# A stick-breaking encoder layer on one core: the down projection in seven products instead of eight, its operands kept in DRAM and moved by GpSimd's queue, and the loops written out

## Chip, core and metric

The kernel runs on one core of one Trainium2 chip. The metric is the device time of one execution in microseconds (us): for the kernel before, the median of 3 runs is 2521.99 us (2521.57 to 2523.63).

## What is computed

One encoder layer for 528 prompt rows (16 of them learned meta rows) and 32 sample rows, all in float32. Only the last part, the SwiGLU block, is touched in its arithmetic:

```python
def layer(h, attend, conv_state, w_in, w_out, ...):          # h: rows x 2048
    xn = rms_norm(h, g_pre_mix); proj = xn @ w_in            # 6144 columns: q k v, gate_b gate_c conv_in
    attn = attend(q, k, v)                                   # stick-breaking attention, 8 heads of 128
    conv_y = short_conv(gate_c * conv_in, conv_state, conv_w)
    mix = concat(group_rms_norm(attn), group_rms_norm(gate_b * conv_y))
    h = h + rms_norm(mix @ w_out, g_post_mix)
    xf = rms_norm(h, g_pre_ffn)
    ff = silu(xf @ w_gate) * (xf @ w_up)                     # w_gate, w_up: 2048 x 5632
    return h + rms_norm(ff @ w_down, g_post_ffn)             # w_down: 5632 x 2048
```

## The kernel before

**Layout.** Activations are kept transposed: 128 channels on the partitions, rows along the free axis. The feed-forward part works on 544 rows (the meta rows are dropped), as two halves of `TH` = 272. Every float32 operand of TensorE is split into a rounded part (`_hi`, made by ScalarE) and a rest (`_lo`, made by VectorE), and each product of a 128x128 weight block is three matmuls: hi x hi, hi x lo, lo x hi.

**Order of the program.** Input projection and mixers (loops `Fori` over pairs of heads and of channel groups), output projection (a loop over pairs of output chunks), then the feed-forward part, in which every instruction is already written out: 44 *steps* of gate and up, then down. Each engine runs its own list in order and waits on semaphores; the order on each engine is written by hand.

**Gate and up: seven products.** A step makes one 256-column block of `w_gate` (even step) or `w_up` (odd step) times the activations, in the Winograd form of Strassen's scheme: the 2x2 blocks of weights and of activations are combined so that 7 products of half-size blocks take the place of 8. The seven products of a step are called, in order, B11, B21, T2, T3, T1, T4, B22. B blocks come straight from the loaded panel, T blocks are differences that VectorE makes (`combine`). Each product uses a tile of 128x1024 weights: ScalarE rounds it (`tile_high`), VectorE makes the rest (`tile_rest`), TensorE then runs 24 matmuls of 272 columns (`product`, line 955). There are 4 tile slots (`RING_T`), so the tile of a product is made only when the product four before it is done. The quarters of the result are finished on VectorE as `c11`, `c22`, `c21`, with the help of copies (`m1`, `u2`, `m7`) that ScalarE takes out of PSUM. Product B22 adds onto the PSUM bank that `c22` reads, so TensorE waits for `c22_made` before B22, the last product of a step.

**The hidden activations.** After an odd step, in the next even step, VectorE multiplies up by gate into `hid` (2 x 544 per partition), ScalarE rounds it to `hid_hi` (`round_hidden`), VectorE makes `hid_lo` (`hidden_rest`), and SyncE stores both to DRAM (`store_hidden`, 2 x 544 KB, lines 573 and 574).

**Down: eight products' worth.** `down_tiles` are 88 tiles of 512x256 weights (`down_raw`, 512 KB), in 4 batches over the 5632 hidden channels. A tile takes 48 matmuls of 272 columns (line 1004). The hidden operand of a batch, `ffs`, is loaded back from DRAM (line 600, 1088 KB each) in bursts on SyncE's queue, ahead of weight tiles on the same queue. At the end of a batch VectorE adds PSUM into `y` (`take_down`, line 1855). In the last batch ScalarE squares finished chunks of `y` and GpSimd adds the squares up (line 1893) for the last norm; the residual `h2_back` (4352 KB) is loaded on SyncE's queue (line 626).

## Time and profile before

| | |
|---|---|
| median of 3 runs | 2521.99 us |
| the profiled execution | 2524.61 us, its span 2522.9 us |
| mean granted TensorE clock | 0.981 |
| TensorE matmul busy | 2440.0 us (97%) |
| VectorE, ScalarE, GpSimd busy | 1252.4, 915.5, 99.0 us |
| moved by DMA | 290.66 MB, mean 115 GB/s |

The span is one execution by the hardware profiler. In rows of groups, the busy time of a matmul group counts overlapping matmuls more than once, since one starts every 0.126 us and lasts 0.29 us; the pace is read from a count over a stretch. An instruction on VectorE or ScalarE lets the next one start some 0.08 to 0.09 us before its own end is recorded.

### The profile page before, as it was taken

How to read it: one execution, taken by the hardware profiler on the slowest of the kernel's cores; microseconds unless marked ns; L12 is line 12 of the kernel's file. 1: busy time of each engine (PE TensorE's matmuls, PEld its weight loads, DVE VectorE, ACT ScalarE, POOL GpSimd, SP SyncE). 2: the span in 40 equal slices, each digit the busy share in tenths (PEclk: the TensorE clock that was granted, in tenths of full speed). 3: DMA queues.
4: the chain of work that ended last, by engine and by line, in shares of the span. 5: the costliest groups of instructions: out<-in, count | busy, mean ns of one | idle time of the engine just before them, and what ended most of it. 6: DMA issues, size and time to landing. Idle time of an engine off the chain costs nothing.

```text
span 2522.9 us, 43292 instructions
## 1 busy us (share of the span) xinstructions
PE 2440.0 (97%) x18716; PEld 2394.1 (95%) x18716; DVE 1252.4 (50%) x1387; ACT 915.5 (36%) x1177; POOL 99.0 (4%) x155
## 2 busy tenths in 40 slices
PE   8999999999999985999999999999999999999997
PEld 7999999999999984999999999999999999999996
DVE  5324332444353228777777767676765222222144
ACT  6344444422342224444444444444443111111123
POOL 0000000000011100000000000000000000000024
PEclk9999999999999996999999999999999999999997
DMA  7223222232225321434343434333336516242222
GB/s 235 83 64 89 80 80 65 85 92 84 80 70 167 89 75 64 134 119 136 118 137 118 137 118 136 119 131 124 126 129 262 187 43 232 76 171 85 105 93 71
DMA packets 313049, 290.66 MB, mean 115 GB/s; under 512 B 8348, under 2 KB 296500, under 8 KB 309956
## 3 DMA queue, kind: packets, MB, share of 16 engines
q1 hardware_dynamic: 298528, 281.70, 34.5%
q10 hardware_dynamic: 14372, 6.77, 0.9%
q8 instruction: 118, 1.93, 0.3%
q14 instruction: 31, 0.25, 0.0%
HBM read 245.82 MB, written 42.61 MB: 114 GB/s over the span
## 4 chain that ended last, share of the span: by engine, by line
PE 90%; DVE 5%; DMA 2%; ACT 2%; SPq 1%; issue 1%; POOL 0%; POOLq 0%; ACTq 0%; DVEq 0%
PE ps L955 36%; PE ps L422 30%; PE ps L1004 19%; PE ps L722 4%; DMA down_raw<-in_w_down_dram 2%; DVE xs L1716 1%; PE ps L666 1%; DMA misc<-in_x_sample_dram 0%; DVE misc L1720 0%; DVE y_left L1880 0%; DVE wide L1685 0%; DVE misc L1689 0%; DVE y_right L1880 0%; ACT xs L1320 0%; DVE t_lo L1695 0%
## 5 line engine op out<-in xcount | busy, mean ns | idle before, releaser
L955 PE MATMUL ps<-xs,t_hi 128*128 128x272 f32 x4928 | 940.5, 291 | 33.1 <-DVE xs L1716 19.1
L955 PEld LDWEIGHTS ps<-xs,t_hi 128*128 128x128 f32 x4928 | 780.9, 190 | 34.7 <-issue 32.2
L955 PE MATMUL ps<-xs,t_lo 128*128 128x272 f32 x2464 | 716.6, 291 | 0.0
L1004 PE MATMUL ps<-ffs,t_hi 128*128 128x272 f32 x2816 | 470.7, 290 | 12.7 <-DVE y_right L1855 7.3
L955 PEld LDWEIGHTS ps<-xs,t_lo 128*128 128x128 f32 x2464 | 467.3, 190 | 0.0
L1695 DVE TENSOR_TENSOR t_lo<-panel,t_hi 128x1024 fp32r<-128x1024 f32 x261 | 319.4, 1224 | 255.7 <-ACT t_hi L1313 255.7
L422 PE MATMUL ps<-act_hi,w_hi 128*128 128x272 f32 (+1 forms) x2048 | 435.4, 294 | 3.5 <-DVE act_lo L1532 2.3
L422 PE MATMUL ps<-act_lo,w_hi 128*128 128x272 f32 (+1 forms) x2048 | 427.0, 290 | 0.0
L422 PE MATMUL ps<-act_hi,w_lo 128*128 128x272 f32 (+1 forms) x2048 | 426.8, 290 | 0.0
L1004 PEld LDWEIGHTS ps<-ffs,t_hi 128*128 128x128 f32 x2816 | 402.2, 190 | 13.4 <-issue 7.5
L1313 ACT CAST t_hi<-panel 128x1024 fp32r<-128x1024 f32 x261 | 272.8, 1045 | 191.8 <-PE ps L955 185.4
L422 PEld LDWEIGHTS ps<-act_hi,w_hi 128*128 128x128 f32 x2048 | 322.8, 189 | 7.5 <-DVE act_lo L1532 3.0
L422 PEld LDWEIGHTS ps<-act_hi,w_lo 128*128 128x128 f32 x2048 | 324.2, 189 | 0.0
L422 PEld LDWEIGHTS ps<-act_lo,w_hi 128*128 128x128 f32 x2048 | 323.8, 189 | 0.0
L1004 PE MATMUL ps<-ffs,t_lo 128*128 128x272 f32 x1408 | 293.3, 290 | 0.0
L1791 DVE TENSOR_TENSOR t_lo<-down_raw,t_hi 128x1024 fp32r<-128x1024 f32 x88 | 109.8, 1248 | 304.1 <-ACT t_hi L1358 304.1
L408 DVE TENSOR_TENSOR w_lo<-w_raw,w_hi 128x1024 fp32r<-128x1024 f32 x126 | 157.9, 1254 | 192.2 <-ACT w_hi L402 190.7
L1358 ACT CAST t_hi<-down_raw 128x1024 fp32r<-128x1024 f32 x88 | 92.2, 1048 | 403.2 <-PE ps L1004 305.8
L402 ACT CAST w_hi<-w_raw 128x1024 fp32r<-128x1024 f32 x128 | 133.7, 1046 | 282.8 <-PE ps L422 222.1
L1004 PEld LDWEIGHTS ps<-ffs,t_lo 128*128 128x128 f32 x1408 | 221.7, 190 | 0.0
L1346 ACT ACTIVATE m<-ps 128x272 f32<-128x272 f32 x88 | 34.9, 397 | 150.1 <-PE ps L955 150.1
L1313 ACT CAST t_hi<-t_raw 128x1024 fp32r<-128x1024 f32 x44 | 46.2, 1049 | 69.3 <-PE ps L955 69.3
(174 smaller groups left out, 1547.1 us busy)
## 6 DMA issues: line engine op xcount, KB each, us to landing
w_raw<-in_w_in_dram SPq DMA_DIRECT2D x96, 512.0 KB, 3.8
panel<-in_w_up_dram SPq DMA_DIRECT2D x44, 1024.0 KB, 5.1
down_raw<-in_w_down_dram SPq DMA_DIRECT2D x88, 512.0 KB, 5.2
panel<-in_w_gate_dram SPq DMA_DIRECT2D x43, 1024.0 KB, 6.4
w_raw<-in_w_out_dram SPq DMA_DIRECT2D x32, 512.0 KB, 3.9
ff_hi_scr<-hid_hi SPq DMA_DIRECT2D x22, 544.0 KB, 2.7
ff_lo_scr<-hid_lo SPq DMA_DIRECT2D x22, 544.0 KB, 4.4
ffs<-ff_hi_scr SPq DMA_DIRECT2D x11, 1088.0 KB, 11.7
```

What stands on the lines that cost most here:

```text
L402: nc.scalar.copy(w_hi[:, k % SLOTS, :], raw_slot(k)).then_inc(hi_ready, 1)
L408: engine.tensor_tensor(w_lo[:, k % SLOTS, :], raw_slot(k), w_hi[:, k % SLOTS, :].bitcast(F32), ALU.subtract).then_inc(lo_ready, 1)
L422: mm = nc.tensor.matmul(out[:, h, :], w[:, k, col:col + width], x[:, x_at + k, token + h * half:token + (h + 1) * half], start=begins, sto ...
L666: return nc.tensor.transpose(out, src, ident[0:n, 0:n])
L722: return nc.tensor.matmul(out, w, x, start=start, stop=True, skip_group_check=True)
L955: mm = nc.tensor.matmul(out, w[:, k, :], xs[:, x, part, k, :], start=begins and k == 0 and w is hi and part == 0, stop=k == KH - 1 and w i ...
L1004: mm = nc.tensor.matmul(ps[:, 4 * (pair % 2) + 2 * n + h, 0:TH], w[:, k, n * P:(n + 1) * P], ffs[:, b % 2, u, part, k, h * TH:(h + 1) * TH ...
L1313: nc.scalar.copy(tile_of(t_hi, i), raw_tile(i)).then_inc(tile_hi, 1)
L1346: A(out[:, :], step_bank(step, letter), ACT.Copy).then_inc(made, 1)
L1358: nc.scalar.copy(down_tile_of(t_hi, i), down_raw[d % 6][:, :, :]).then_inc(tile_hi, 1)
L1695: V.tensor_tensor(tile_of(t_lo, i), raw_tile(i), tile_of(t_hi, i).bitcast(F32), ALU.subtract) .then_inc(tile_lo, 1)
L1791: V.tensor_tensor(down_tile_of(t_lo, i), down_raw[d % 6][:, :, :], down_tile_of(t_hi, i).bitcast(F32), ALU.subtract).then_inc(tile_lo, 1)
```

## The change

1. **Down in seven products.** Down becomes 24 steps (`DSTEPS`): 6 batches of 4 or 3 pairs of hidden chunks (`KBS`), 4 column blocks each. A step has the same seven products as gate and up, each with a tile of 128x1024 (batches of 4) or 128x768 (batches of 3), and 24 or 18 matmuls of 272 columns. Weights come through the same panels as gate and up (`load_panel`, 1 MB or 0.75 MB), and VectorE makes four differences for each step as before. After every product VectorE takes 2x272 columns out of PSUM into `y` (`take_down`), since the next product adds on in the same bank.
2. **Seven hidden operands.** Down needs seven combinations of the hidden quarters, not two. VectorE makes four more quarters (`hidden_sums`), and rounding, rest and stores work on 7x272 = 1904 elements per partition instead of 1088. Each store is 128 x 7 pieces of 1088 bytes, 0.975 MB; two for each pair of steps. `hid_lo` now lies on top of `hid`, so `c11` of an odd step waits until the stores have landed (`hid_stored`).
3. **Places.** `round_hidden` moves behind the `m7` copy in the even step, `hidden_rest` to the odd step behind `combine(T4)`, and `c11` of odd steps behind the tile of B22.
4. **Queue.** Stores and loads of hidden operands are issued by GpSimd; loads of `xd` (12 slots, 2 x 544 KB each) begin as products of the last step free their room, and later follow the last use of a slot.
5. **Loops.** Every `Fori` becomes a Python loop.

```diff
-        with sp.Fori(0, HEADS // 2 - 1) as r:          # and so for all engines and loops
+        for r in range(0, HEADS // 2 - 1):
...
+    KBS = [4, 4, 4, 4, 3, 3]
+    NQ = KC // 4
+    DSTEPS = NQ * len(KBS)
+    ALL = STEPS + DSTEPS
+    XD = 12
...
             def round_hidden(j):
-                act.wait_ge(hid_made, j + 1)
+                act.wait_ge(hid_summed, 4 * (j + 1))
                 if j:
                     act.wait_ge(hid_stored, 32 * j)
                 nc.scalar.copy(hid_hi[:, :, :], hid[:, :, :]).then_inc(hid_rounded, 1)
...
-                if is_gate and step:
-                    round_hidden(j - 1)
                 copy_out(u2, step, T2, "a", u2_copied, c21_made)
                 tile_high(7 * step + 6)
                 copy_out(m7, step, T3, "b", m7_copied, c22_made)
+                if is_gate and step:
+                    round_hidden(j - 1)
                 tile_high(ahead)
...
             def c11(step):
-                if step >= 2:
-                    dve.wait_ge((hid_made, hid_split)[step % 2], step // 2)
+                if step >= 2 and step % 2 == 0:
+                    dve.wait_ge(hid_made, step // 2)
+                if step >= 3 and step % 2:
+                    dve.wait_ge(hid_stored, 32 * (step // 2))
...
+            def hidden_sums(j):
+                d21, d11, d12, d22, s1, s2, s4 = (hid[:, h, :] for h in range(7))
+                dve.wait_ge(hid_made, j + 1)
+                V.tensor_tensor(s1, d21, d22, ALU.add).then_inc(hid_summed, 1)
+                dve.wait_ge(hid_summed, 4 * j + 1)
+                V.tensor_tensor(d21, d11, d21, ALU.subtract).then_inc(hid_summed, 1)
+                V.tensor_tensor(s2, s1, d11, ALU.subtract).then_inc(hid_summed, 1)
+                dve.wait_ge(hid_summed, 4 * j + 3)
+                V.tensor_tensor(s4, d12, s2, ALU.subtract).then_inc(hid_summed, 1)
...
+            for d in range(DSTEPS):                      # TensorE
+                b, m = d // NQ, d % NQ
+                for q in range(7):
+                    i = 7 * (STEPS + d) + q
+                    slot = (7 * b + q) % XD
+                    pe.wait_ge(tile_lo, i + 1)
+                    if m == 0:
+                        pe.wait_ge(xd_loaded[slot], 32 * ((7 * b + q) // XD + 1))
...
+                    in_y = {B11: 7 * (d - 1), B21: 7 * (d - 1) + 2, T2: 7 * d + 1, T3: 7 * (d - 1) + 6,
+                            T1: 7 * d + 3, T4: 7 * d + 4, B22: 7 * d + 5}[q]
+                    if in_y > 0:
+                        pe.wait_ge(y_added, in_y)
+                    for n in range(2):
+                        for k in range(KBS[b]):
+                            for w, part in ((hi, 0), (hi, 1), (lo, 0)):
+                                mm = nc.tensor.matmul(out[:, n, :], w[:, k, n * P:(n + 1) * P], xd[:, slot, part, k, :], ...
...
+            def store_hidden(j):                         # GpSimd
+                pool.wait_ge(hid_split, j + 1)
+                for part, src in enumerate((hid_hi, hid_lo)):
+                    pool.dma_start(ff_scr[part][:, :, j, :], src[:, :, :].bitcast(F32)).then_inc(hid_stored, 16)
...
+            for j in range(FF // 2 - 1):
+                store_hidden(j)
+            for i in range(XD):
+                pool.wait_ge(product_done, 7 * LAST + i // 2 + 1)
+                load_hidden(i)
+            store_hidden(FF // 2 - 1)
+            for i in range(XD, 7 * len(KBS)):
+                b, q = (i - XD) // 7, (i - XD) % 7
+                pool.wait_ge(product_done, 7 * (STEPS + NQ * b + NQ - 1) + q + 1)
+                load_hidden(i)
```

The order of instructions moves at three places. First, ScalarE's list in an even (gate) step, from the copy of `u2` or the tile ahead of it to the first two tiles of the next step (`m`, `u` are the copies `m1`, `m7`, `u2`; panels carry a buffer number). Before:

```order
L1313 CAST t_hi<-panel_69 128x1024
L1352 CAST hid_hi<-hid 128x1088
L1346 ACTIVATE u_73<-ps 128x272
L1313 CAST t_hi<-panel_69 128x1024
L1346 ACTIVATE m_74<-ps 128x272
L1313 CAST t_hi<-panel_70 128x1024
L1313 CAST t_hi<-panel_68 128x1024
```

After:

```order
L1332 ACTIVATE u_73<-ps 128x272
L1299 CAST t_hi<-panel_69 128x1024
L1332 ACTIVATE m_74<-ps 128x272
L1338 CAST hid_hi<-hid 128x1904
L1299 CAST t_hi<-panel_70 128x1024
L1299 CAST t_hi<-panel_68 128x1024
```

The rounding of the hidden operand stood ahead of the copy of `u2`; now it stands behind the `m7` copy and directly ahead of the tile of the next step's B11, and it is 1904 elements wide instead of 1088.

Second, VectorE's list in the same even step, from the tile of T4 to `c22` (which is `gate<-ps,m_74`). Before:

```order
L1695 TENSOR_TENSOR t_lo<-panel_69,t_hi 128x1024
L1759 TENSOR_TENSOR gate<-ps,m_72 128x272
L1695 TENSOR_TENSOR t_lo<-panel_69,t_hi 128x1024
L1786 TENSOR_TENSOR hid_lo<-hid,hid_hi 128x1088
L1695 TENSOR_TENSOR t_lo<-panel_70,t_hi 128x1024
L1708 TENSOR_TENSOR panel_70<-panel_70 128x8x128
L1764 TENSOR_TENSOR gate<-ps,m_74 128x272
```

After:

```order
L1674 TENSOR_TENSOR t_lo<-panel_69,t_hi 128x1024
L1741 TENSOR_TENSOR gate<-ps,m_72 128x272
L1674 TENSOR_TENSOR t_lo<-panel_69,t_hi 128x1024
L1769 TENSOR_TENSOR hid<-hid 128x272
L1771 TENSOR_TENSOR hid<-hid 128x272
L1772 TENSOR_TENSOR hid<-hid 128x272
L1774 TENSOR_TENSOR hid<-hid 128x272
L1674 TENSOR_TENSOR t_lo<-panel_70,t_hi 128x1024
L1688 TENSOR_TENSOR panel_70<-panel_70 128x8x128
L1747 TENSOR_TENSOR gate<-ps,m_74 128x272
```

The rest of the hidden operand left this step, and four sums of 272 elements stand in its place. They come ahead of the tile of the next step's B11.

Third, VectorE's list in the next odd (up) step, from the tile of T3 to `c22` (here `hid<-ps,m_74`). Before:

```order
L1695 TENSOR_TENSOR t_lo<-panel_70,t_hi 128x1024
L1708 TENSOR_TENSOR panel_68<-panel_68,t_raw 128x8x128
L1695 TENSOR_TENSOR t_lo<-panel_70,t_hi 128x1024
L1695 TENSOR_TENSOR t_lo<-panel_68,t_hi 128x1024
L1759 TENSOR_TENSOR hid<-ps,m_72 128x272
L1695 TENSOR_TENSOR t_lo<-panel_68,t_hi 128x1024
L1695 TENSOR_TENSOR t_lo<-panel_69,t_hi 128x1024
L1708 TENSOR_TENSOR panel_69<-panel_69 128x8x128
L1764 TENSOR_TENSOR hid<-ps,m_74 128x272
```

After:

```order
L1674 TENSOR_TENSOR t_lo<-panel_70,t_hi 128x1024
L1688 TENSOR_TENSOR panel_68<-panel_68,t_raw 128x8x128
L1778 TENSOR_TENSOR hid_lo<-hid,hid_hi 128x1904
L1674 TENSOR_TENSOR t_lo<-panel_70,t_hi 128x1024
L1674 TENSOR_TENSOR t_lo<-panel_68,t_hi 128x1024 x2
L1741 TENSOR_TENSOR hid<-ps,m_72 128x272
L1674 TENSOR_TENSOR t_lo<-panel_69,t_hi 128x1024
L1688 TENSOR_TENSOR panel_69<-panel_69 128x8x128
L1747 TENSOR_TENSOR hid<-ps,m_74 128x272
```

The rest of the hidden operand now stands ahead of the tiles of T1 and T4, and `c11` (`hid<-ps,m_72`), which carries the wait for the stores, behind the tile of B22; the tile of the next B11, `combine(T1)` and `c22` stand behind it.

## Rows read from the trace of the kernel before

**Rows 1.** The page: busy time by engine; the chain that ended last, by line

```profile
PE 2440.0 (97%) x18716; PEld 2394.1 (95%) x18716; DVE 1252.4 (50%) x1387; ACT 915.5 (36%) x1177; POOL 99.0 (4%) x155
...
PE ps L955 36%; PE ps L422 30%; PE ps L1004 19%; PE ps L722 4%; DMA down_raw<-in_w_down_dram 2%; DVE xs L1716 1%; PE ps L666 1%; DMA misc<-in_x_sample_dram 0%; DVE misc L1720 0%; DVE y_left L1880 0%; DVE wide L1685 0%; DVE misc L1689 0%; DVE y_right L1880 0%; ACT xs L1320 0%; DVE t_lo L1695 0%
```

**Rows 2.** Stretches: us, busy of PE, PEld, DVE, ACT, POOL (x instructions), clock, DMA, GB/s

```profile
40.00:860.00 820.00, 816.17 (x6179) 790.67 (x6179) 302.64 (x415) 314.13 (x376) 45.82 (x113) 1.00 0.30 89
1100.00:1970.00 870.00, 870.00 (x6903) 870.00 (x6902) 609.89 (x640) 374.94 (x500) 0.00 (x0) 1.00 0.42 142
```

**Rows 3.** The chain in order of time, down and the end

```profile
1937.94 144.34 PE ps L1004 x1152
...
2085.43 17.78 DMA down_raw<-in_w_down_dram
...
2380.07 14.79 DMA down_raw<-in_w_down_dram
...
2485.82 0.73 DVE y_right L1855
2486.58 0.67 ACT y_sq L1122
```

**Rows 4.** PE's waits, 2000 to 2523 us

```profile
PE ps L1004 <- DVE y_right L1855: 7.3, 1, 7.3
PE ps L1004 <- DVE t_lo L1791: 5.3, 1, 5.3
```

**Rows 5.** Groups by form: busy us, mean ns of one, idle before

```profile
L1695 DVE TENSOR_TENSOR t_lo<-panel,t_hi 128x1024 fp32r<-128x1024 f32 x261 | 319.4, 1224 | 255.7 <-ACT t_hi L1313 255.7
...
L1313 ACT CAST t_hi<-panel 128x1024 fp32r<-128x1024 f32 x261 | 272.8, 1045 | 191.8 <-PE ps L955 185.4 <-DMA panel<-in_w_up_dram 6.5
...
L1893 POOL TENSOR_TENSOR y_sq_sum<-y_sq_sum,y_sq 128x544 f32<-128x544 f32 x14 | 19.0, 1354 | 63.9 <-ACT y_sq L1122 63.8
...
L1855 DVE TENSOR_TENSOR y_right<-ps,y_right 128x544 f32<-128x544 f32 x24 | 17.3, 724 | 44.8 <-PE ps L1004 44.8
...
L1716 DVE TENSOR_TENSOR xs<-misc,xs 128x2176 fp32r<-128x2176 f32 x6 | 14.4, 2422 | 3.9 <-ACT xs L1320 3.9
...
L1320 ACT CAST xs<-misc 128x2176 fp32r<-128x2176 f32 x6 | 11.9, 2004 | 20.6 <-DVE misc L1746 9.0 <-DVE misc L1720 6.9 <-DVE t_lo L1695 4.7
```

**Rows 6.** Timeline of DVE: start us, duration us, line, operation

```profile
1525.83 1.28 DVE L1786 TENSOR_TENSOR hid_lo<-hid,hid_hi 128x1088 fp32r<-128x1088 f32 x1
1527.72 1.23 DVE L1695 TENSOR_TENSOR t_lo<-panel,t_hi 128x1024 fp32r<-128x1024 f32 x1 [0.60 <-ACT t_hi L1313]
1528.86 1.22 DVE L1708 TENSOR_TENSOR panel<-panel 128x1024 f32<-128x1024 f32 x1
1529.99 0.43 DVE L1764 TENSOR_TENSOR gate<-ps,m 128x272 f32<-128x272 f32 x1
...
1537.94 1.22 DVE L1708 TENSOR_TENSOR panel<-panel,t_raw 128x1024 f32<-128x1024 f32 x1
1539.82 1.23 DVE L1695 TENSOR_TENSOR t_lo<-panel,t_hi 128x1024 fp32r<-128x1024 f32 x1 [0.67 <-ACT t_hi L1313]
```

**Rows 7.** Timeline of ACT, the same steps

```profile
1526.64 1.04 ACT L1313 CAST t_hi<-panel 128x1024 fp32r<-128x1024 f32 x1
...
1535.43 0.40 ACT L1340 ACTIVATE gate<-ps 128x272 f32<-128x272 f32 x1 [1.65 <-PE ps L955]
```

**Rows 8.** Timeline of SP's DMA issues, the same steps

```profile
1527.19 0.34 SPq L573 DMA_DIRECT2D ff_hi_scr<-hid_hi  x1
1527.57 0.43 SPq L574 DMA_DIRECT2D ff_lo_scr<-hid_lo  x1
1528.05 13.41 SPq L560 DMA_DIRECT2D panel<-in_w_gate_dram  x2
```

**Rows 9.** Stretches with transfers, columns as in rows 2

```profile
1527.75:1534.50 6.75, 6.75 (x56) 6.75 (x55) 6.75 (x8) 3.08 (x5) 0.00 (x0) 1.00 0.94 317
1942.00:1946.00 4.00, 4.00 (x34) 4.00 (x33) 1.67 (x2) 1.05 (x1) 0.00 (x0) 1.00 1.04 397
```

**Rows 10.** DMA issues of line 600: ns min/median/max

```profile
L600 SPq DMA_DIRECT2D ffs<-ff_hi_scr x11: 319/432/5236, 1919.8 to 2235.5; - x11
```

**Rows 11.** The page's DMA issues: KB each, us to landing

```profile
panel<-in_w_up_dram SPq DMA_DIRECT2D x44, 1024.0 KB, 5.1
...
ff_hi_scr<-hid_hi SPq DMA_DIRECT2D x22, 544.0 KB, 2.7
```

More of the change, by code:

```diff
@@ L582, in _ @@
                     sp.wait_ge(tile_lo, T1 + 1)
-                if step > 3 and step % 2 == 0:
-                    store_hidden(step // 2 - 2)
                 load_panel(step, 0)
@@ L889, in _ @@
                 head(0, u, u, u > 0, False)
-            with pe.Fori(1, HEADS // 2) as p:
+            for p in range(1, HEADS // 2):
                 for u in range(2):
@@ L894, in _ @@
                 group(HEADS // 2, u, HEADS + u, first_pair=True)
-            with pe.Fori(HEADS // 2 + 1, (HEADS + GROUPS) // 2) as p:
+            for p in range(HEADS // 2 + 1, (HEADS + GROUPS) // 2):
                 for u in range(2):
@@ L930, in _ @@
             two_chunks(T_OUT, mix_chunk, 2, {6: last_norm_and_rows})
-            with pe.Fori(1, KC // 2) as q:
+            for q in range(1, KC // 2):
                 for c in range(2):
@@ L1246, in _ @@
                 head(0, u, u, u > 0, False)
-            with act.Fori(1, HEADS // 2) as p:
+            for p in range(1, HEADS // 2):
                 for u in range(2):
@@ L1251, in _ @@
                 group(HEADS // 2, u, HEADS + u, first_pair=True)
-            with act.Fori(HEADS // 2 + 1, (HEADS + GROUPS) // 2) as p:
+            for p in range(HEADS // 2 + 1, (HEADS + GROUPS) // 2):
                 for u in range(2):
@@ L1294, in _ @@
             out_round(0, 2)
-            with act.Fori(1, KC // 2 - 1) as q:
+            for q in range(1, KC // 2 - 1):
                 out_round(q, 0)
@@ L1635, in _ @@
                 head(0, u, u, u > 0, False)
-            with dve.Fori(1, HEADS // 2) as p:
+            for p in range(1, HEADS // 2):
                 for u in range(2):
@@ L1640, in _ @@
                 group(HEADS // 2, u, HEADS + u, first_pair=True)
-            with dve.Fori(HEADS // 2 + 1, (HEADS + GROUPS) // 2) as p:
+            for p in range(HEADS // 2 + 1, (HEADS + GROUPS) // 2):
                 for u in range(2):
@@ L1673, in _ @@
             out_round(0, 2)
-            with dve.Fori(1, KC // 2 - 1) as q:
+            for q in range(1, KC // 2 - 1):
                 out_round(q, 0)
@@ L1802, in _ @@
                     x_rest(S3, 6, a21)
+                if step % 2 and step > 1:
+                    hidden_rest(step // 2 - 1)
                 tile_rest(7 * step + 4)
@@ L1818, in _ @@
                     c11(step)
+                if step % 2:
+                    c11(step)
                 if after_up:
-                    hidden_rest(step // 2 - 1)
-                if step < LAST:
+                    hidden_sums(step // 2 - 1)
+                tile_rest(ahead)
+                combine(step + 1, T1)
+                c22(step)
+                combine(step + 1, T2)
+                tile_rest(ahead + 1)
+                c21(step)
+                combine(step + 1, T3)
+                tile_rest(ahead + 2)
@@ new lines, in _ @@
+            for d in range(DSTEPS):
+                step = STEPS + d
+                ahead = 7 * (step + 1)
+                more = step + 1 < ALL
+                if d:
+                    take_down(d - 1, B22)
+                tile_rest(7 * step + 3)
+                combine(step, T4)
+                if d == 0:
+                    times_gate(LAST)
+                if d == 1:
+                    hidden_rest(FF // 2 - 1)
+                take_down(d, B11)
+                tile_rest(7 * step + 4)
+                if d == 0:
+                    times_gate_rest(LAST)
+                take_down(d, B21)
+                tile_rest(7 * step + 5)
+                take_down(d, T2)
+                tile_rest(7 * step + 6)
+                if d == 0:
+                    hidden_sums(FF // 2 - 1)
+                take_down(d, T3)
+                if more:
@@ L1925, in mask @@
                 last.then_inc(ready, 1)
-            with pool.Fori(1, HEADS + 1) as heads:
+            for heads in range(1, HEADS + 1):
                 mask(relu, sp_made, sp_ready, heads)
```

299 lines of the change are left out of this document (120 added, 179 removed).

## The prediction

> **What bounds the kernel now.** I read the page first: TensorE is busy 97% of the span, and nine tenths of the chain that ended last are its matmuls [rows 1]. A busy PE can hide small gaps, so the next view is the windows: from 1100 to 1970 us, inside gate and up, PE is busy 870 of 870 us with 6903 matmuls, 0.126 us each, at clock 1.00 [rows 2]. So a product of 24 matmuls takes 3.02 us and a step of 168 takes 21.17 us. VectorE (610 of 870 us) and ScalarE (375) follow. Whatever removes matmuls gains, and whatever makes PE wait between products loses, one for one. The chain in order of time shows down from 1937.94 to 2485.82 us, 547.9 us [rows 3]; its 4224 matmuls at 0.126 are 532 us, and PE waited 7.3 and 5.3 us [rows 4], once behind a burst of hidden operands and once behind the residual, each time with `down_raw` late on the same queue [rows 3]. The sum is made against the profiled execution's parts (span 2522.9, own time 2524.61) and applied to the median 2521.99, 2.6 us below it.
>
> **Down itself.** Seven products of 2 x K x 3 matmuls, 4 column blocks, the K adding up to 22: 7 x 2 x 3 x 22 x 4 = 3696 matmuls, 528 fewer. At 0.126 us, with the same 272 columns, 465.7 us. Is VectorE able to follow? A 1024-wide operation starts 1.14 us after the one before it (1527.72 to 1528.86 [rows 6]); one of 272 takes 0.35 by the same slope, the 544 taken out of PSUM 0.64 (0.724 recorded [rows 5], less the 0.08 overlap). A step of K = 4 asks 7 rests, 4 differences and 7 takes: 11 x 1.14 + 7 x 0.64 = 17.0 us of 21.17. A step of K = 3 (768 wide, 0.87): 11 x 0.87 + 7 x 0.64 = 14.0 of 15.9. The tightest slot holds a take, a rest and a difference: 2.92 of 3.02 us, and 2.38 of 2.27 us for K = 3. There VectorE slips 0.1 us a slot, plus 0.5 where the rest must first wait for ScalarE's rounding, and gains it back in the three slots without a difference. PE needs a take only two products after its own, so with K = 3 it may be 1.6 us late; I find at most 0.8. No stall. The two old waits go too: weights and hidden operands no longer stand behind each other in one queue. The residual still goes ahead of panels, 11 us at 397 GB/s [rows 9], but a panel is issued about 16 us ahead of its use.
>
> At the start of down the first seven slots (7.8 MB) are issued behind the last store, together with three panels; at 350 to 397 GB/s they arrive 0 to 5 us late for the last product of the first step; I take 2. The sums and the rounding of the last hidden pair stand in this step as well, 1.2 us. Down: 465.7 + 3.2 - 547.9 = **-79.0**.
>
> **The end.** Before, the last take (0.73) and one square (0.67) stand between the last product and the norm [rows 3]. Now the last product finishes two chunks, and the two before them are done one product (2.27 us) earlier: four additions on GpSimd at 1.35 us each [rows 5] run into the end. T4's take and first square end 1.0 us before the last product, two additions bring it to +1.7, the third to +3.1, against 1.4 now: **+1.7**.
>
> **Loops.** Between 40 and 860 us, where most loops run, PE is idle 3.8 us in all [rows 2]. Written out they give 0 to 3.8; code that is written out already runs without a gap from 1100 us on, so I add no price for it. **-0.5**.
>
> **Even steps: a new wait behind the sums.** The even step shown ends at 1535.4 (ScalarE answers B22 at 1535.43 [rows 7]), so its B22 starts at 1532.35. Today `c22` runs at 1529.99 and ends at 1530.42 [rows 6], 1.9 us early. In the change four sums start where the rest stood, at 1525.83. Two wait for an earlier one's end (0.43 + 0.06), so the last ends at 1527.6. ScalarE then rounds 1904 elements: between 1045 ns for 1024 and 2004 for 2176 [rows 5] that is 1.78 us, 1.69 until the next may start. The tile of the next B11 starts at 1529.35 instead of 1526.64 [rows 7]. Behind it, one after the other without slack, stand the rest, `combine(T1)` and `c22` [rows 6]. So `c22` ends at 1533.13, and B22 waits **0.83 us**. 21 even steps: **+17.4**. Its bounds are 0.5 and 1.2 (a semaphore wait more or less on each hop), 10 to 25 us.
>
> **Odd steps: the store.** VectorE comes 1 to 2 us late out of the even step, so `combine(T4)`, 2.5 us after the step's start now (1537.94 [rows 6]), runs at about 3.0, and the rest of 1904 elements (2.13 us, between 1.22 and 2.42 [rows 5]) ends at 6.25. Then two stores of 0.975 MB go out. `c11` waits for both, and behind it in VectorE's list stand the tile of the next B11, `combine(T1)` and `c22`: 0.35 + 1.14 + 1.14 + 0.43 + 0.1 of hops = 3.2 us. B22 starts at 18.15. So the stores have 8.7 us from the end of the rest; each microsecond more costs PE one, 21 times.
>
> How long do they take? Before, two stores of 0.557 MB and one panel half (1.05 MB) share the engines: 317 GB/s from 1527.75 to 1534.5, ramps included [rows 9], first bytes some 0.8 us after the issue at 1527.19 [rows 8]. In the change the panel half is issued by SyncE 1.1 us behind the stores (its condition, the tile of T1, is next in VectorE's list), and runs beside them on the other queue, so it must be moved before the stores are through: 3.0 MB. At 397 GB/s, the rate of large pieces [rows 9], this is 7.6 us, at 317 it is 9.5. I take 350, 8.6 us, since the pieces are 1088 bytes: more than the weights' 1024, less than the 4352 of the old stores. With 0.1 for the hop, 0.8 to the first byte, 0.5 for a queue that no row shows and 0.3 for the end: 10.3 us, **1.6 us** late, 21 times: **+33.6**. Bounds: 8.5 us (no wait at all, +0), and 13.3 us, if each of GpSimd's issues of 896 pieces takes as long as the longest issue of line 600, 5.24 us [rows 10], and a landing of 2.7 [rows 11] follows: 4.6 us late, +97.
>
> The Trainium skill (DMA: Bandwidth & Descriptors, Anatomy of one DMA) gives 2.0 us + bytes / 436 GB/s for a DMA issued from GpSimd, and calls the making of descriptors small. By it, 3.0 MB would be through in 8.9 us, 0.2 us late, and the whole kernel at an estimated 2466 us: the rival below called "hidden". No row here shows a DMA issued by GpSimd. The same page (Issuing engines are not separate DMA queues) says that all queues run on the same 16 engines, so that another issuer saves issue time only; it speaks for counting the panel with the stores.
>
> **Sum.** -79.0 + 1.7 - 0.5 + 17.4 + 33.6 = -26.8: **2495 us**, 1.1% less.
>
> **Rivals.**
> - *Hidden* (25%): the stores are through in under 9.3 us, because they and the panel run at the 397 GB/s of large pieces. For it: in down the old queue held 397 GB/s over 4 us with weights and hidden operands mixed [rows 9]. Then the odd steps cost 0 to 13 us: 2521.99 - 79.0 + 1.7 - 0.5 + 17.4 = 2462 to 2475.
> - *GpSimd is slow to issue* (25%), the case on the other side: seven pieces for each partition, 896 in each of the two DMAs, must be written out before the engines can move them, and SyncE's issues do not show this cost. It decides from 11.6 us on, where 21 waits of 2.9 us eat the whole gain: 2523. At 13.3 us the time is 2559. Against it: SyncE issues the 1024 pieces of a panel half with no such delay, and it lands in 5.1 us [rows 11].
> - *Down is bound by VectorE* (5%): each take or semaphore hop 0.2 us dearer than the rows give, so that the K = 3 steps fall behind: 8 steps by 1 to 2 us, 10 to 16 us more than forecast, 2505 to 2511.
> - The rest, 45%, is the forecast, 2478 to 2515.
>
> **How the numbers follow.** Runs of one kernel differ by under 0.1%, a comparison can tell about 0.2%, 5 us. Slower by more than that is the upper part of the slow issuer, 24%; within it, where forecast and slow issuer meet (2517 to 2527), 7%; faster 69%. The range: 2458 (hidden, with all of the loops' 3.8 us) to 2560 (the upper bound of the stores). It holds both sides, since the stores' time multiplies by 21.
>
> **What the profile would show.** Right: 3696 matmuls in down in about 470 us at full busy; in gate and up, PE idle 0.8 us before the last product of even steps, released by `gate<-ps,m`, and 1 to 2 us before that of odd steps, released by `hid<-ps,m`; VectorE's `c11` in odd steps waiting on the transfer into `ff_lo_scr`, 10 us after GpSimd's issue. Wrong: a landing far from 10 us; a step of 21.2 us or of more than 24; PE waiting for `y_left`, `y_right` or `xd` within down. The forecast falls if GpSimd's queue delays more than the 0.5 us given it, or if the engines serve the stores before the panel.

## The result

The changed kernel takes **2606.18 us** (median of 4 runs, 2602.51 to 2609.05) against 2522.81 (2521.57 to 2525.19) for the kernel before on the same chip: ratio **1.0328**, 95% interval 1.031 to 1.0347. It is slower by 83 us where 27 us less were forecast, and the time lies above the range. The profiled execution of the changed kernel has a span of 2600.8 us; the differences below are made against the 2522.9 of before.

The page of the changed kernel, busy time by engine, then the chain by line (they answer to [rows 1]):

```profile
PE 2424.8 (93%) x18188; PEld 2369.7 (91%) x18188; DVE 1553.0 (60%) x1755; ACT 1009.2 (39%) x1257; POOL 189.3 (7%) x283
...
PE ps L427 29%; PE ps L938 15%; PE ps L995 15%; DMA ff_lo_scr<-hid_lo 9%; PE ps L705 4%; DVE t_lo L1674 4%; DVE panel L1688 3%; ACT t_hi L1299 3%; DVE hid_lo L1778 2%; DMA panel<-in_w_down_dram 1%; PE ps L649 1%; POOL ff_hi_scr L1953 1%; DVE xs L1696 1%; DVE misc L1700 0%; DVE y_left L1888 0%
```

The matmuls of gate and up (now line 938) no longer hold the chain alone: 9% of it is a transfer, the second store of the hidden operand. TensorE's waits in the changed kernel (in total, times, longest) say where:

```profile
PE ps L938 <- DVE hid L1747: 82.3, 21, 6.7
...
PE ps L938 <- DVE gate L1747: 18.1, 21, 0.9
```

These are the waits for `c22`, from the end of the last matmul to the start of the next, in the odd steps (3.9 us each; 1.6 forecast) and in the even ones (0.86 each; 0.83 forecast). What `c22` is late for in an odd step is in VectorE's waits, and in the page's DMA issues (KB each, us to landing; before: [rows 11]):

```profile
DVE hid L1741 <- DMA ff_lo_scr<-hid_lo: 143.8, 20, 9.9
```

```profile
panel<-in_w_gate_dram SPq DMA_DIRECT2D x43, 1024.0 KB, 7.2
...
ff_hi_scr<-hid_hi POOLq DMA_DIRECT2D x22, 952.0 KB, 6.1
ff_lo_scr<-hid_lo POOLq DMA_DIRECT2D x22, 952.0 KB, 11.5
```

One odd step in time, first VectorE, then GpSimd, then SyncE's queue (start, duration):

```profile
1521.08 2.14 DVE L1778 TENSOR_TENSOR hid_lo<-hid,hid_hi 128x1904 fp32r<-128x1904 f32 x1
...
1536.12 0.44 DVE L1741 TENSOR_TENSOR hid<-ps,m 128x272 f32<-128x272 f32 x1 [7.12 <-DMA ff_lo_scr<-hid_lo]
```

```profile
1523.54 0.91 POOL L1953 DMA_DIRECT2D ff_hi_scr<-hid_hi  x1 [45.03 <-DVE hid_lo L1778]
1524.27 1.11 POOL L1953 DMA_DIRECT2D ff_lo_scr<-hid_lo  x1
```

```profile
1524.38 0.37 SPq L585 DMA_DIRECT2D panel<-in_w_gate_dram  x1
1529.02 0.37 SPq L585 DMA_DIRECT2D panel<-in_w_up_dram  x1
```

The rest ends at 1523.2, the store has landed at 1536.0: **12.8 us**, where 10.3 were forecast. GpSimd begins its first issue 0.3 us after the rest and takes 0.7 us to the next; from then to the landing it is 11.7 us. Behind `c11` the tail of 3.2 us is as forecast (1536.12 to TensorE's restart at 1539.33).

The second thing is in the granted clock. Stretches of TensorE around this wait (us, busy of PE, PEld, DVE, ACT, POOL, then clock, DMA share, GB/s), with the long stretches that answer to [rows 2]:

```profile
1100.00:1970.00 870.00, 787.52 (x5916) 780.84 (x5915) 579.55 (x635) 347.78 (x442) 33.03 (x36) 0.95 0.38 124
1535.40:1539.30 3.90, 0.04 (x1) 0.01 (x1) 3.18 (x5) 0.79 (x1) 0.00 (x0) 0.88 0.41 143
1539.30:1545.00 5.70, 5.67 (x25) 5.70 (x26) 4.77 (x5) 1.05 (x1) 0.00 (x0) 0.50 0.01 3
2200.00:2300.00 100.00, 100.00 (x795) 100.00 (x795) 82.60 (x85) 34.69 (x33) 7.47 (x14) 1.00 0.55 184
```

After 3.9 us without a matmul, TensorE works for 5.7 us at a clock of 0.50, the level of 1.2 GHz: 25 matmuls where the usual pace gives some 45. The page shows this as busy time, which is why "93% busy" and "5916 matmuls in 870 us instead of 6903" are both true.

What the slow clock costs can be read from one wait to the next. In gate and up a wait stands before every B22, so 168 matmuls lie between TensorE's restart after one wait and the start of the next wait. Behind the short waits of even steps this takes 21.42 us each time. Behind the waits of two odd steps it took (the clock is the mean of the stretch):

```profile
1539.33:1563.35 24.02, 24.02 (x168) 23.80 (x168) 16.05 (x20) 10.22 (x12) 0.00 (x0) 0.88 0.28 89
1589.12:1612.06 22.94, 22.93 (x168) 22.72 (x168) 16.05 (x20) 10.23 (x12) 0.00 (x0) 0.93 0.29 92
```

The same reading for all 21 odd steps gives 1.3 to 2.7 us beyond 21.42, **41.3 us** in all, 2.0 for each pair of steps.

**Where the 78 us are.** Down starts at 2088.40 instead of 1937.94, 150.5 us later. Of this, 82.3 + 18.1 are the waits above. The 50 us left are not waits; 41.3 of them are the slow clock, the rest is placed further below. Down then takes from 2088.40 to 2556.9, 468.5 us instead of 547.9: -79.4. From the last product to the end it is 43.9 us instead of 37.1: +6.8. Sum: 150.5 - 79.4 + 6.8 = 77.9, the difference of the spans.

### The profile page after: what moved, and what is told of

Its sections match the earlier page's. It is cut to its first block, busy times and chain, and to the rows that moved or that the text cites. A ratio compares the mean times of both kernels' runs of the same rounds, so it can differ in the third digit from the quotient of the medians.

```text
span 2600.8 us, 42070 instructions
## 1 busy us (share of the span) xinstructions
PE 2424.8 (93%) x18188; PEld 2369.7 (91%) x18188; DVE 1553.0 (60%) x1755; ACT 1009.2 (39%) x1257; POOL 189.3 (7%) x283
## 4 chain that ended last, share of the span: by engine, by line
PE 64%; DVE 15%; DMA 11%; ACT 5%; issue 5%; POOL 1%; SPq 0%; DVEq 0%; ACTq 0%; POOLq 0%
PE ps L427 29%; PE ps L938 15%; PE ps L995 15%; DMA ff_lo_scr<-hid_lo 9%; PE ps L705 4%; DVE t_lo L1674 4%; DVE panel L1688 3%; ACT t_hi L1299 3%; DVE hid_lo L1778 2%; DMA panel<-in_w_down_dram 1%; PE ps L649 1%; POOL ff_hi_scr L1953 1%; DVE xs L1696 1%; DVE misc L1700 0%; DVE y_left L1888 0%
## 5 line engine op out<-in xcount | busy, mean ns | idle before, releaser
L938 PE MATMUL ps<-xs,t_hi 128*128 128x272 f32 x4928 | 983.5, 299 | 132.4 <-DVE hid L1747 82.3
L938 PEld LDWEIGHTS ps<-xs,t_hi 128*128 128x128 f32 x4928 | 813.8, 198 | 141.8 <-issue 139.4
L1674 DVE TENSOR_TENSOR t_lo<-panel,t_hi 128x1024 fp32r<-128x1024 f32 (+1 forms) x405 | 486.1, 1200 | 232.7 <-ACT t_hi L1299 226.6
L1299 ACT CAST t_hi<-panel 128x1024 fp32r<-128x1024 f32 (+1 forms) x405 | 412.1, 1023 | 492.2 <-PE ps L995 232.6
L995 PE MATMUL ps<-xd,t_hi 128*128 128x272 f32 x2464 | 466.4, 289 | 3.6 <-DVE y_left L1839 1.5
L995 PEld LDWEIGHTS ps<-xd,t_hi 128*128 128x128 f32 x2464 | 387.3, 188 | 4.9 <-issue 4.9
L995 PE MATMUL ps<-xd,t_lo 128*128 128x272 f32 x1232 | 356.6, 289 | 0.0
L995 PEld LDWEIGHTS ps<-xd,t_lo 128*128 128x128 f32 x1232 | 231.7, 188 | 0.0
L1299 ACT CAST t_hi<-t_raw 128x1024 fp32r<-128x1024 f32 (+1 forms) x68 | 69.7, 1025 | 145.4 <-DVE t_raw L1688 110.1
L1953 POOL DMA_DIRECT2D ff_hi_scr<-hid_hi x22 | 20.0, 910 | 1136.1 <-DVE hid_lo L1778 1136.1
```

The costliest lines, as they stand in the source:

```text
L938: mm = nc.tensor.matmul(out, w[:, k, :], xs[:, x, part, k, :], start=begins and k == 0 and w is hi and part == 0, stop=k == KH - 1 and w i ...
L995: mm = nc.tensor.matmul(out[:, n, :], w[:, k, n * P:(n + 1) * P], xd[:, slot, part, k, :], start=q in (B11, B21, T3) and k == 0 and w is h ...
L1299: nc.scalar.copy(tile_of(t_hi, i), raw_tile(i)).then_inc(tile_hi, 1)
L1674: V.tensor_tensor(tile_of(t_lo, i), raw_tile(i), tile_of(t_hi, i).bitcast(F32), ALU.subtract)\
L1953: pool.dma_start(ff_scr[part][:, :, j, :], src[:, :, :].bitcast(F32)).then_inc(hid_stored, 16)
```

## The experiments

The expectations speak of theories. The main one: the stores of an odd step land later than forecast, the long wait lowers the clock as well, and together they eat the gain of down; all else went as forecast. What lengthens the landing was then divided into "bytes beside a panel half" (D) and "GpSimd's many pieces by themselves" (E). Each kernel is the changed one with the edit shown, unless told otherwise.

### Who issues: stores on SyncE's queue

```diff
                 load_panel(step, 0)
+                if step % 2 == 0 and 4 <= step <= STEPS + 2:
+                    store_hidden(step // 2 - 2)          # SyncE; GpSimd's is gone
```

> The changed kernel with one thing undone: the two stores of the hidden operand are issued by SyncE, ahead of the second panel half of the next step, instead of by GpSimd. Theory A (the loss is the wait of c11 in odd steps for the stores, 3.9 us each, and the lower clock that follows it, about 2.4 us each, 21 times, and it comes from sharing the engines with two panel halves and from GpSimd's later start): in one queue the stores go first, land 6 to 8 us after the rest is made, the wait and the low clock go, 2606 - 21 x 6.3 = about 2474 us. Rival B (the amount moved in that window decides, whoever issues it): the landing stays over 10 us and the time over 2550 us. Rival C (the panel halves behind the stores come late instead): ScalarE waits for the panel, 2480 to 2520 us.

2501.71 us, ratio to before 0.9915 (0.9898 to 0.9931): the gain is there, but less than the 2474 of the main theory. Its trace, the second store's issues, then TensorE's waits:

```profile
ff_lo_scr<-hid_lo SPq DMA_DIRECT2D x22, 952.0 KB, 7.7
```

```profile
PE ps L945 <- DVE hid L1754: 20.1, 5, 19.0
```

In the odd steps the second store lands 7.7 us after its issue and TensorE hardly waits (1.1 us in the other four waits together). One wait of 19.0 us stands at the last step ahead of down, where this kernel issues the last stores while GpSimd's 24 loads of hidden operands are under way (1940 to 1985 us):

```profile
xd<-ff_lo_scr POOLq DMA_DIRECT2D x12, 544.0 KB, 17.0
...
ff_lo_scr<-hid_lo SPq DMA_DIRECT2D x1, 952.0 KB, 27.3
```

So this edit does two things: it puts the panel half behind the stores in one queue, and it opens a new collision. It doesn't say which of issuer and order mattered. The time lies in the range of rival C, but not for its reason: the late step is that of the last stores, not a step with a late panel half.

### Who waits: `c22` of odd steps in a buffer of its own

```diff
-                if step >= 3 and step % 2:                                 # in c11
-                    dve.wait_ge(hid_stored, 32 * (step // 2))
...
+                out = up22[:, :] if step % 2 else quarter(gate, 1, 1)      # in c22
...
+                if step >= 3 and step % 2:                                 # in c21
+                    dve.wait_ge(hid_stored, 32 * (step // 2))
...
-                if step % 2:
-                    c11(step)                        # behind the tile of B22
...
                 c21(step)
+                if step % 2:
+                    c11(step)
```

> The changed kernel, GpSimd still issuing, with the wait moved off the path: in odd steps c22 goes into a spare buffer, c11 stands behind c21, and c21 carries the wait for the stores. Theory A: the stores still take 12 to 13 us, but nothing waits for long; no wait of TensorE in odd steps, clock 1.00, about 2474 us. Rival: if transfers by GpSimd slow the kernel in another way (panel halves late, ports), more than 20 us of the 132 stay, over 2495 us.

**2480.05 us**, ratio 0.983 (0.9814 to 0.9846). The stores are as slow as before (the trace shows 11.6 us), but nothing on TensorE's way waits for them, and the clock stays at 1.00 from 1100 to 1935 us. TensorE's waits for `c22`:

```profile
PE ps L939 <- DVE gate L1747: 18.6, 22, 0.9
```

Against the changed kernel, 126 us: 21 waits of 3.9 us are 82 of them. This shows that the whole loss hangs on that one wait, and that the other 44 us of it are no waiting time: with the wait gone, the slow clock goes as well.

### The wait shortened: `c11` two entries later

```diff
-                if step % 2:
-                    c11(step)
...
                 tile_rest(ahead)
                 combine(step + 1, T1)
+                if step % 2:
+                    c11(step)
                 c22(step)
```

> The changed kernel, in which c11 of odd steps, with its wait for the stores, stands behind the tile of the next B11 and combine(T1) instead of ahead of them. TensorE's wait should fall from 3.9 to about 1.7 us each, 21 times. If the lower clock after it follows from any wait of this kind, 2606 - 46 = about 2560 us; if a wait of 1.7 us leaves the clock at 1.00, as the 0.86 us of even steps does, about 2606 - 46 - 50 = 2510 us.

2522.47 us, ratio 0.9996 (0.9985 to 1.0008). The wait is not removed, only shortened:

```profile
PE ps L938 <- DVE hid L1747: 37.1, 21, 4.3
```

```profile
1100.00:1970.00 870.00, 820.73 (x6382) 813.48 (x6381) 625.76 (x684) 374.18 (x475) 34.94 (x38) 0.99 0.41 135
```

21 waits of 1.8 us on average instead of 3.9 save 45.2 us of waiting, but 83.7 us of time; of the spans, 2600.8 - 2524.0 = 76.8. The other **31.6 us** are slow clock that this kernel is spared, but it isn't spared all of it, as the mean of 0.99 says. After two of its waits, of 1.5 and of 2.3 us, the 168 matmuls took

```profile
1089.36:1110.78 21.42, 21.42 (x168) 21.20 (x168) 16.05 (x20) 10.24 (x12) 0.00 (x0) 1.00 0.32 101
1135.37:1158.28 22.91, 22.91 (x168) 22.68 (x168) 16.05 (x20) 10.22 (x12) 0.00 (x0) 0.93 0.28 94
```

In six of the 21 odd steps the clock fell to 0.50 for a while, after waits of 1.8 to 4.3 us; after the other 15, of 1.0 to 1.7 us, it stayed at 1.00. The length alone doesn't decide: it also stayed at 1.00 after single waits of 2.5 us (the last kernel but one below, at 1939.7) and 2.8 us (the one with long runs, at 1974.1). The six cost 8.8 us, 1.3 to 1.5 each. So 41.3 us in the changed kernel less 8.8 here are 32.5, and agree with the 31.6 from the times. Both expectations missed: 2560 supposed that all of the clock loss stays, 2510 that all of it goes and that nothing but the clock made up the 50 us.

### What makes the landing late: each panel half held back

Two halves of a panel are issued near the stores: the second half of the next gate panel, 0.1 us behind the second store, and the first half of the up panel, 4.6 us later. Three kernels hold one, the other, or both until the stores have landed:

```diff
                 load_panel(step, 0)
+                if step % 2 and 5 <= step <= STEPS + 1:           # ahead of load_panel(step, 0)
+                    sp.wait_ge(hid_stored, 32 * ((step - 2) // 2))
...
+                if step % 2 == 0 and 4 <= step <= STEPS:          # ahead of load_panel(step, 1)
+                    sp.wait_ge(hid_stored, 32 * (step // 2 - 1))
                 load_panel(step, 1)
```

The first half held (the upper addition alone):

> The changed kernel, in which SyncE holds the first panel half of the step after next back until the stores of this odd step have landed. It has 14 us to spare. Theory A: 1.05 MB less shares the window, the landing falls from 12.8 to about 10.3 us, TensorE's wait in odd steps from 3.9 to about 1.4 us. If a wait of 1.4 us still lowers the clock, about 2553 us; if it doesn't, about 2503 us. Rival (pieces of 1088 bytes or GpSimd's issuing limit the stores, not sharing): landing and time as in the changed kernel, 2606 us.

The second half held (the lower one alone):

> Of the two panel halves around the stores only the second half of the odd step's own panel (issued 0.1 us beside the stores) is held until the stores have landed; the first half of the next one goes as in the changed kernel. Theory D (bytes of the stores beside bytes of that one half are what lengthens the landing): ff_lo lands 7.0 us after issue as with both halves held, the wait of TensorE in odd steps is under 0.5 us each, time 2485 to 2495. Rival (it takes both halves, or either will do): ff_lo stays at 10 us or more and the time stays near 2600.

Both held:

> The changed kernel, in which SyncE holds both panel halves back until the stores of an odd step have landed, so that no transfer shares their window; TensorE waits for panels then, and only the landing of the stores is read. Theory D (loads beside the stores cost more than their own bytes: reading and writing at once moves 230 to 290 GB/s where either alone moves about 400): ff_lo lands 6 to 7.5 us after its issue instead of 11.7. Rival E (GpSimd's queue with 7 pieces for each partition is slow by itself): it lands 9.5 us or later.

Landing of the second store, first half held, second half held, both held:

```profile
ff_lo_scr<-hid_lo POOLq DMA_DIRECT2D x22, 952.0 KB, 11.6
```

```profile
ff_lo_scr<-hid_lo POOLq DMA_DIRECT2D x22, 952.0 KB, 7.0
```

The first line is of the first kernel, the second stands in both others. Times: 2599.39 (ratio 1.0304, 1.0285 to 1.0323), **2494.31** (0.9887, 0.9871 to 0.9904), and 2489.55 in one run. My expectation for the first, that this half takes the stores' bandwidth, missed altogether. It is the second half alone, 4.6 us on the landing. Two stretches of one microsecond in the changed kernel, 4.0 and 5.0 us behind the first issue (us, TensorE busy, clock, DMA share, GB/s):

```profile
1527.50:1528.50 1.00, 1.00 (x11) 1.00 1.01 237
1528.50:1529.50 1.00, 1.00 (x11) 1.00 1.06 227
```

and with the stores alone:

```profile
1518.40:1519.40 1.00, 1.00 (x10) 1.00 1.02 370
1519.40:1520.40 1.00, 1.00 (x10) 1.00 1.02 370
```

The engines are busy all the time in both, but move 227 to 237 GB/s in the changed kernel, less than the stores alone (370) and less than panel halves alone (365 to 373 in each microsecond from 1526.4 to 1529.4 in the kernel with both held). Who moves what is in the packets by queue; q0 is GpSimd's, with the stores, q1 SyncE's, with the panels (packets, MB, share of the 16 engines). The changed kernel from 1528.5 to 1530.5 us:

```profile
q1 hardware_dynamic: 471, 0.48, 88.5%
q0 software_dynamic: 24, 0.03, 8.2%
```

and the stores alone from 1518.4 to 1520.4 us, as long after their first issue:

```profile
q0 software_dynamic: 185, 0.74, 101.8%
```

So it is not a sharing by halves. At first the stores go ahead, and the load hardly moves (0.07 MB from 1526.5 to 1528.5); then, between the first store and the second, GpSimd's queue all but stands still for two microseconds, and only the panel half moves. Such a stretch of two microseconds, with under 0.03 MB of stores, is in the trace in 20 of the 21 odd steps that wait, so it makes up near half of the 4.6 us. (In the other one GpSimd issues its second store 6.2 us after the first instead of 0.7, and TensorE waits 6.7 us, the longest of all; why this issue is late is not known.) Where the first half is held, the same standstill is there, with the second half beside it. In the five microseconds behind it the stores' queue moves the same in either kernel, whatever runs beside it. The changed kernel from 1530.5 us, then the one with the first half held from 1527.5 us:

```profile
q1 hardware_dynamic: 1016, 1.02, 58.3%
q0 software_dynamic: 239, 0.97, 47.3%
```

```profile
q0 software_dynamic: 238, 0.97, 47.8%
q1 hardware_dynamic: 571, 0.57, 35.1%
```

That is why holding the first half back won nothing on the landing.

### The length of a piece

```diff
-        ff_scr = [nc.dram_tensor(f"ff_{part}_scr", (P, 7, FF // 2, TH), F32, kind="Internal").ap()
+        ff_scr = [nc.dram_tensor(f"ff_{part}_scr", (P, FF // 2, 7, TH), F32, kind="Internal").ap()
```

A store is then one run of 7616 bytes for each partition instead of seven of 1088.

> The changed kernel with the DRAM tensors laid out so that a store writes one run of 7616 bytes for each partition instead of 7 pieces of 1088, and a load reads pieces of 1088 bytes instead of one run of 4352. If the small pieces make the stores slow (225 to 296 GB/s in their first 4 us), they land 2 to 4 us sooner, and the time falls to 2500 to 2560 us. If sharing is all, the landing stays within 1 us and the time within 20 us of 2606 us, and loads in down may land later without a wait.

**2486.31 us**, ratio 0.9854 (0.9837 to 0.9871), with the stores on GpSimd's queue and the panel half beside them: 14 us below the lower end of what I expected, since the landing fell by more than the 2 to 4 us allowed. The same layout with both halves held back:

> The layout of one 7616-byte run per partition, and both panel halves held until the stores have landed. Theory D in its simple form (a load beside them always costs the stores): ff_lo lands in 5.5 us or less instead of 7.3. Rival (with long runs the load beside them costs the stores nothing, only short pieces suffer from it): 7.0 to 7.3 us as before. Time near 2485 in both, since the wait of the odd steps is gone already.

2486.93 us in one run. Landings, first beside the half, then alone:

```profile
ff_lo_scr<-hid_lo POOLq DMA_DIRECT2D x22, 952.0 KB, 7.3
```

```profile
ff_lo_scr<-hid_lo POOLq DMA_DIRECT2D x22, 952.0 KB, 5.8
```

| second store lands after | alone | beside the panel half |
|---|---|---|
| pieces of 1088 bytes | 7.0 us | 11.6 us |
| runs of 7616 bytes | 5.8 us | 7.3 us |

Short pieces cost 1.2 us alone and 4.3 beside a load. Neither pure theory holds: it is the two together. In the kernel with long runs the queues share as follows from 1518.4 to 1520.4 us, again 4.9 us behind the first issue; the stores' queue does not stand still there:

```profile
q0 software_dynamic: 62, 0.46, 96.8%
q1 hardware_dynamic: 57, 0.06, 8.2%
```

The edit changes more than the length in DRAM: in the profile two stores of short pieces are 448 packets of 4352 bytes, four pieces each, and two of long runs 256 of 7616 (with 32 small ones in both). These runs don't tell which of the two counts. GpSimd's issue is shorter too, as the page of the kernel with long runs and, for the changed kernel, its own page show:

```profile
L1953 POOL DMA_DIRECT2D ff_hi_scr<-hid_hi x22 | 11.9, 541 | 1036.5 <-DVE hid_lo L1778 1036.5
```

```profile
L1953 POOL DMA_DIRECT2D ff_hi_scr<-hid_hi x22 | 20.0, 910 | 1136.1 <-DVE hid_lo L1778 1136.1
```

Last, long runs with SyncE as issuer (both edits):

> Stores issued by SyncE ahead of the second panel half, in the layout of long runs. If the layout and the issuer are two remedies of the same wait, nothing is left to win in the odd steps: ff_lo lands in under 7.3 us, and what is left is the late start of down that the kernel with SyncE stores showed (a wait of 19.0 us, 2501.7): time 2495 to 2503. Rival (that late start came from the slow bytes of the last stores too): it shrinks to under 8 us and the time is 2483 to 2490.

2486.99 us, ratio 0.986 (0.9844 to 0.9877), the same as with GpSimd (0.9854), and as the rival had it. Once the runs are long, the issuer makes no difference that these runs can tell. For short pieces the issuer alone was not changed: with SyncE the order changed as well. And the late start of down shrinks from 19.0 to 5.3 us:

```profile
PE ps L945 <- DVE hid L1754: 5.3, 1, 5.3
```

### The loops, the even steps, and all together

The kernel before, with its 13 loops written out and nothing else:

```diff
-        with sp.Fori(0, HEADS // 2 - 1) as r:
+        for r in range(0, HEADS // 2 - 1):
```

> The kernel before with its 13 loops written out and nothing else. The prediction gave this 0 to 3.8 us of gain, -0.5 in the sum; the two traces show TensorE equally busy from 40 to 860 us (816 of 820). All theories: within 2 us of the kernel before.

2524.87 us, ratio 1.0002 (0.9993 to 1.0012): no effect.

The spare buffer for `c22`, and in even steps the rounding one place later:

```diff
+                tile_high(ahead)
                 if is_gate and step:
                     round_hidden(j - 1)
-                tile_high(ahead)
                 tile_high(ahead + 1)
```

> The variant with c22 in a spare buffer, and in even steps ScalarE rounds the hidden operand behind the tile of the next B11 instead of ahead of it. The wait for gate<-ps,m (0.86 us, 21 times) should go and nothing else: 2480 - 18 = 2462 us, and PE's wait for DVE gate under 2 us. Rival: the later rounding makes the tile of the next B21 late and gives a part back, 2466 us or more.

**2453.33 us**, ratio 0.9724 (0.9708 to 0.974), the best of all. The wait for `gate` is gone, and the stretch within gate and up is back at 0.126 us a matmul:

```profile
1100.00:1950.00 850.00, 847.50 (x6719) 847.18 (x6719) 659.02 (x722) 386.66 (x499) 49.35 (x64) 1.00 0.46 151
```

It gains 26.7 us on the kernel without this edit, 8 more than the 18.6 us of wait that it removes and 9 below the 2462 expected. The starts of `c22` in even steps, first and last of 22, show why (with the wait, then without):

```profile
L1747 DVE TENSOR_TENSOR gate<-ps,m x22: 434/434/435, 1022.1 to 1934.9; 128x272 f32<-128x272 f32 x22
```

```profile
L1747 DVE TENSOR_TENSOR gate<-ps,m x22: 431/434/436, 1021.9 to 1910.7; 128x272 f32<-128x272 f32 x22
```

A pair of steps takes (1934.9 - 1022.1) / 21 = 43.47 us with the wait and 42.32 without, so a wait of 0.86 us costs 1.15 (22 x 1.15 = 25.3). The first 0.16 of the other 0.3 is the last matmul before the wait: it lasts 0.29 us, where the next one would have started after 0.126. The remaining 0.1 is spread over the restart; the runs show its size, not its cause. The odd steps agree: without waits 168 matmuls take 42.32 / 2 = 21.16 us, and from a restart to the next wait they take 21.42 with the clock at 1.00, after short and long waits alike. So each wait costs 0.26 to 0.29 us beyond its length.

Both, and long runs:

> Long runs, the spare buffer for c22, and the rounding of hidden behind the next high tile, all in one. Free c22 with the later rounding had no wait of TensorE left in gate and up (2453.3); long runs can then only take the odd slow microsecond out of down's start: 2448 to 2454. Rival (loads of hidden from long-run layout are slower, 11.4 and 13.8 us against 9.9 and 11.6, and that shows in down): 2455 to 2462.

2457.46 us, ratio 0.9742 (0.9726 to 0.9759), not faster than without the long runs; the intervals overlap, and the time is above the 2448 to 2454 expected. The loads back are slower from that layout (the page shows 11.6 and 14.4 us for the two parts here, 9.8 us for the first without it), as the rival had it (that this is what sets the time was not tested), and the faster stores no longer have anyone waiting.

## Why the prediction was wrong

- **Down: right.** 468.5 us against 465.7 + 3.2 = 468.9; -79.4 against -79.0. VectorE follows, TensorE is busy 100.00 of 100 us (x795) in the middle of it. In part this is luck: of the 3.2 us, 2 were for hidden operands that arrive late, and no wait for them is in the trace. TensorE waits 3.4 us in down, all for `y_left` and `y_right`, which the prediction had named as a sign of being wrong.
- **Loops: right**, nothing.
- **Even steps: the wait was right (0.86 against 0.83), its price was not.** It costs 0.3 us more than it lasts: 24 us for 21 of them instead of 17.4.
- **Odd steps: the step that failed, twice.** First, "3.0 MB", "I take 350, 8.6 us", and with it 10.3 us to the landing. It is 12.8. The hop to GpSimd is 0.3, not 0.1, and the issues themselves are near what was allowed. The time for the bytes is what was mis-sized: one rate for both transfers was taken from large pieces and from the old stores [rows 9], which are 4352 bytes long, while in fact the stores' queue stands still for about two microseconds beside the panel half. The prediction named "if the engines serve the stores before the panel" as a way to fail; here they served the panel before the second store. The argument that a length of 1088 is "more than the weights' 1024" was wrong, since loads of 1024-byte pieces do well by themselves [rows 11], and stores of 1088 bytes alone nearly so (7.0 us), but not both at once (11.6). With the stores alone the wait would have been gone, as in the rival "hidden". The wait became 3.9 us, 82.3 in all, inside the bounds of 0 to 97. The rival "GpSimd is slow to issue" named about the right landing from the wrong cause: an issue takes 0.9 and 1.1 us, not 5.2, and SyncE with the same bytes in long runs is no faster than GpSimd.
- **Second, the missing term: TensorE's clock.** The sum took a wait of TensorE at its own length ("each microsecond more costs PE one"). At 3.9 us it isn't: the engine comes back at 0.50, or falls to it soon after, and loses 2.0 us more for each pair, 41.3 us in all. The restarts, 42 x 0.26 = 10.9 us, come on top. The kernel before also lost 3.8 us that the changed one doesn't, in one wait early in gate and up: 2.0 for the wait, 0.3 for the restart and 1.5 for the clock behind it. Its wait, and TensorE's stretches during and after it:

```profile
PE ps L955 <- DVE gate L1764: 2.0, 1, 2.0
```

```profile
1020.20:1022.10 1.90, 0.00 (x0) 0.00 (x0) 1.80 (x3) 0.00 (x0) 0.00 (x0) 1.00 0.89 303
1022.10:1025.00 2.90, 2.86 (x13) 2.89 (x14) 0.89 (x1) 0.83 (x1) 0.00 (x0) 0.53 1.08 361
```

So 41.3 + 10.9 - 3.8 = 48.4 of the 50.1 us that are no waits have a place. The Trainium skill (TensorE: Matmul & The Clock Gate, HAM oscillation) describes such kernels, where each wait for a transfer ends with the array at half its rate; the trace agrees, with 0.50 from 1539.3 to 1545.0. A price for the clock should have stood beside the upper bound of the stores, which ended at 2560: with 41.3 us more it would have reached 2601, with the restarts 2612.
- **The end: +6.8 against +1.7.** GpSimd's additions ran into the end, as forecast, but three in a row begin behind the last product, the first 1.5 us after it, where the forecast had the first of its three begin 1.0 us before it. In the chain of the changed kernel in order of time (start, us) 5.9 us lie between the last product and the sums over rows, against 1.5 before; and those take 3.57 us, against 1.20 for the same piece before:

```profile
2556.94 0.74 DVE y_right L1839
...
2558.43 1.35 POOL y_sq_sum L1901
...
2559.92 1.34 POOL y_sq_sum L1901
...
2561.39 1.34 POOL y_sq_sum L1901
...
2562.77 3.57 PE ps L699 x8
```

With measured sizes the prediction's sum closes: -79.4 + 6.8 + 18.1 + 82.3 + 10.9 + 41.3 - 3.8 = 76.2, against 77.9. The other 1.7 us stay unplaced.

**Still open.** Why GpSimd's queue stands still between two stores of short pieces when a load is beside them is not shown, only that it does, and that it doesn't without the load and with long runs only in two odd steps. The Trainium skill (DMA: Bandwidth & Descriptors, Queues, rings and completion order) says that a DMA engine takes turns between queues packet by packet. Both transfers are stretched, as turns would have it: in the odd step shown the panel half lands after 10.7 us instead of 5.9. But the trace doesn't show turns in those two microseconds, with 0.48 MB on one queue and 0.03 on the other, and turns alone would keep the total rate, which fell to 227. The same page's sum (Anatomy of one DMA), 2.0 us + bytes / 436 GB/s, gives an estimated 6.5 us for the two stores together. Alone and in long runs they take 0.5 + 5.8 = 6.3 from the first issue, so there the trace agrees; beside the load in short pieces they take 0.7 + 11.6 = 12.3, and there it doesn't hold. The end was not changed in any experiment; its 6.8 us are read from the chain alone.

## What to carry to other kernels

Price a new wait of the bounding engine as its length plus the restart, and look whether the granted clock falls with it, since then it costs half as much again (here 2.0 us more for one of 3.9). Size a transfer by the length of its pieces and by what runs beside it, not by its bytes at another transfer's rate; for one that must land in time, make the pieces long, or hold the load beside it. And before making a late transfer faster, ask who waits for it: one spare buffer of 272 columns (2480.05 us) was worth more here than the best way of speeding up the stores (2486.31).

## What the runs showed of the hardware

- Two stores of 0.975 MB in pieces of 1088 bytes on GpSimd's queue, with a load of 1.05 MB in pieces of 1024 on SyncE's: for two microseconds between the stores their queue moves 0.03 MB and the load's 0.48. The total falls to 227 to 237 GB/s at a DMA share of 1.0; the stores alone reach 370.
- After 3.9 us without a matmul TensorE ran 5.7 us at a clock of 0.50. In the kernel with shorter waits it fell to 0.50 after waits of 1.8 to 4.3 us, six times, and stayed at 1.00 after waits of 0.9 to 1.7; in two other kernels it stayed there after a wait of 2.5 and of 2.8. Such a fall cost 1.3 to 2.7 us.
- A wait between products costs 0.26 to 0.29 us beyond its length, also where the clock stays at 1.00.
- GpSimd's issue of a DMA of 896 pieces is recorded with 0.91 and 1.11 us, one of 128 long runs with 0.54; TensorE's time did not depend on the issuer once the runs were long.
